# Attention: TensorE does the scores of the next pair of heads in front of the transposes of the exponentials

## The chip, the core and the metric

The kernel runs on one core of a Trainium2 chip. The metric is device time in microseconds (us). Three runs of the kernel before gave 1885.36, 1885.52 and 1888.36 us; their median is 1885.52 us.

## The reference

One layer of an encoder is applied to two sequences, a prompt of 512 tokens and a sample of 1024, width 1024. Half of the width goes through a Fourier mix, the other half through attention in a neighbourhood on a grid of 64 columns, with 8 heads of 64 channels. Then come an output projection and a gated feed-forward part. Only the attention matters here:

```python
s = jnp.einsum('bqhd,brqkhd->bqhrk', qi, kc,
               preferred_element_type=jnp.float32) * scale + bias[None]
p = jax.nn.softmax(s.reshape(b, GRID_W, h, kh * WIN_COLS), axis=-1)
p = p.reshape(b, GRID_W, h, kh, WIN_COLS).astype(v.dtype)
return jnp.einsum('bqhrk,brqkhd->bqhd', p, vc)
```

Each query sees 8 rows by 16 columns of keys; the scores get a learned bias, a softmax, and weigh the values.

## The kernel before

The kernel is five stages, one after the other, each a block in which every engine has its own hand-written list of work: first stage, projections, attention, Fourier mix, second half. Engines meet through counting semaphores alone, and each engine takes its list strictly in the order in which it is written.

`attention` (L748) works in 48 units. A unit `w` is a pair of heads, a strip of 16 columns and a chunk of 512 tokens (128 queries): 4 pairs, 4 strips, 3 chunks. Pair and strip together are a "block" `m` of three units, and there are 16 blocks. The first unit of a block has 256 keys, the other two have 384. The loop on each engine has steps `s`; a step works on several units at once:

- `scores(w)` (L947, its matmul is L958) is on TensorE. The two heads of the pair write PSUM banks 0 and 1, and each head first waits until VectorE has read the same bank for unit `w-1` (semaphore `scored`, L951).
- `score(w, hh)` (L881, its operation is L887) is on VectorE. It adds mask and bias, takes the row's extreme, and writes `s_ring`. It waits for the scores in the bank, for the mask from GpSimd (L831), and for the transposes of unit `w-2`, which read the same part of the ring.
- `exp(w, hh)` (L837, L841) is on ScalarE: the exponential in place.
- `turn(w)` (L960, L967) is on TensorE: it transposes the exponentials, 128 keys at a time, into banks 2 and 3; 4 transposes for 256 keys, 6 for 384.
- `copy_pt(w)` copies the transposed exponentials out of PSUM into `pt_ring`: the first head on ScalarE (L849), the second on VectorE (L899).
- `spread(w)` (L971, L976) and `values(w)` (L981, L992) are on TensorE: the reciprocal row sums spread over the partitions, and the product with the values. `scale_out` (L907, VectorE) writes the result.
- `turn_v(m, part)` (L936, L944) on TensorE transposes the values of the next block, staged by GpSimd (L813), through bank 7. Part 0 has four tiles, part 1 two. Part 1 uses the bank again, so it waits until ScalarE has copied part 0 out (`values_ready`, L863). VectorE copies part 1 (L915).

In step `s`, ScalarE does `exp(s, 0)`, `copy_pt(s-1)`, `exp(s, 1)`, in one step of three `values_ready`, then `copy_scale(s-1)`. VectorE does the reciprocal (L892) and `copy_pt` of unit `s-1`, with the output of `s-2` between them, and then both `score(s+1, hh)`. So VectorE's list has the copy of the transposes in front of the next scores. The steps repeat with a period of three; for what follows they are called

- **A** (`s` = 3m): turns a unit of 384 keys, scores one of 384;
- **B** (`s` = 3m+1): turns one of 256, part 0 of `turn_v`, scores one of 384;
- **C** (`s` = 3m+2): turns one of 384, part 1 of `turn_v`, scores one of 256.

Of the kernel before, what the change touches and what calls it, by code (L numbers as in the profile page):

```python
# [55 lines left out]
PAIRS_A = (D_FOURIER // 128) * NB * NCH  # L56
# [691 lines left out]
def attention(nc, at, sem, banks, kept):  # L748
# [28 lines left out]
    def pair_unit(w):  # L777
        p, b, c = w // (NB * NCH), w // NCH % NB, w % NCH
        return p, b, c, KEY_ROWS[c], KEY_ROWS[c] * KCOLS

    def block_at(s, lead):

        m, rest = divmod(s + lead, NCH)
        return m if rest == 0 and 0 < m < BLOCKS else None
# [4 lines left out]
    with nc.Block() as block:  # L789
        @block.sync  # L790
        def _(sp):
            for b in range(NB // 2, NB):
                sp.dma_start(mask[1][:, b - NB // 2], masks[:, MASK_COLS * b:MASK_COLS * b + MASK_COLS]
                             ).then_inc(mask_in[b], 16)
            for p in range(1, FT):
                if p >= 2:
                    sp.wait_ge(masked_bias, 2 * NB * NCH * (p - 1))
                load_bias(sp, rpb_pad, bias[p % 2], bias_in[p % 2], p)
                if p == 1:
                    for r, cols in enumerate((slice(0, T_PROMPT), slice(T_PROMPT, T))):  # L800
                        sp.dma_start(kept.u[:, :, cols], kept.u_scratch[:, cols].rearrange("(g p) t -> p g t", p=128)
                                     ).then_inc(kept.u_in[r], 16)
                    sp.dma_start(kept.cs[:], kept.dft_c).then_inc(kept.cs_in, 16)
                    sp.dma_start(kept.wf[:], kept.w_fmix.rearrange("g c d -> c g d")).then_inc(kept.wf_in, 16)
# [129 lines left out]
        @block.tensor  # L934
        def _(pe):
            def turn_v(m, part):  # L936
                if part:
                    pe.wait_ge(v_act, m + 1)
                else:
                    pe.wait_ge(v_staged, m + 1)  # L940
                    if m:
                        pe.wait_ge(v_dve, m)
                for t in range(4 * part, NVT if part else 4):
                    last = pe.transpose(banks[:, 7, 128 * (t % 4):128 * (t % 4) + 128], v_pair[:, m % 2, 128 * t:128 * t + 128], ident[:])  # L944
                last.then_inc(v_turned, 1)

            def scores(w):  # L947
                p, b, c, rows, n = pair_unit(w)
                for hh in range(2):
                    if w:  # L950
                        pe.wait_ge(scored, 2 * w + hh - 1)  # L951
                    head = slice(64 * hh, 64 * hh + 64)
                    q0 = p * T + c * CH + 128 * b
                    queries = z[head, q0:q0 + 128]
                    k0 = (FT + p) * T + KEY_TOKEN0[c]
                    keys = z[head, k0:k0 + rows * GRID_W].rearrange("p (r w) -> p r w", w=GRID_W)[
                        :, :, KEY_COL[b]:KEY_COL[b] + KCOLS]
                    pe.matmul(banks[:, hh, 0:n], queries, keys, start=True, stop=True).then_inc(qk_done, 1)  # L958

            def turn(w):  # L960
                rows = pair_unit(w)[3]
                for hh in range(2):
                    pe.wait_ge(exped, 2 * w + hh + 1)
                    if w:
                        pe.wait_ge((pt_act, pt_dve)[hh], w)
                    for j in range(rows // 4):
                        last = pe.transpose(banks[:, 2 + hh, 128 * j:128 * j + 128],  # L967
                                            s_ring[:, w % 2, hh, 128 * j:128 * j + 128], ident[:])
                    last.then_inc(p_turned, 1)

            def spread(w):  # L971
                pe.wait_ge(recip_done, w + 1)
                if w:
                    pe.wait_ge(scale_copied, w)
                for hh in range(2):
                    last = pe.matmul(banks[64 * hh:64 * hh + 64, 6, 0:128],  # L976
                                     stats[:, 2, 2 * w + hh:2 * w + hh + 1].broadcast_to((128, 64)), ident[:],
                                     start=True, stop=True)
                last.then_inc(scale_spread, 1)

            def values(w):  # L981
                p, b, c, rows, n = pair_unit(w)
                if c == 0:
                    pe.wait_ge(v_act, NB * p + b + 1)
                    pe.wait_ge(v_dve, NB * p + b + 1)
                pe.wait_ge(pt_act, w + 1)
                pe.wait_ge(pt_dve, w + 1)
                if w >= 2:
                    pe.wait_ge(o_done, w - 1)
                for j in range(rows // 4):  # L990
                    for hh in range(2):
                        last = pe.matmul(banks[64 * hh:64 * hh + 64, 4 + w % 2, 0:128],  # L992
                                         v_tok[:, b * NVT + V_TILE0[c] + j, 64 * hh:64 * hh + 64],
                                         pt_ring[:, w % 2, hh, 128 * j:128 * j + 128], start=(j == 0), stop=(j == rows // 4 - 1))
                last.then_inc(pv_done, 1)
            scores(0)
            turn_v(0, 0)
            turn_v(0, 1)
            for s in range(PAIRS_A + 1):
                if s:  # L1000
                    turn(s - 1)
                for part in range(2):
                    m = block_at(s, 2 - part)
                    if m is not None:
                        turn_v(m, part)
                if s + 1 < PAIRS_A:
                    scores(s + 1)
                if s:
                    spread(s - 1)
                    values(s - 1)  # L1010
# [865 lines left out]
```

## Time and profile before

| what | us |
|---|---|
| median of three runs | 1885.52 |
| the profiled execution, its own time | 1885.33 |
| span of the profiled execution | 1883.5 |
| TensorE busy in that span | 1792.1 (95%) |
| VectorE, ScalarE, GpSimd busy | 853.6, 485.9, 489.0 |
| attention stage, from 398 to 554 | 156.0 |
| TensorE, ScalarE, GpSimd, VectorE busy in that stage | 133.69, 99.29, 97.40, 89.26 |

The span runs from the first to the last instruction; 1.83 us lie around it. An engine's busy time is the union of its instructions; TensorE's overlaps of matmuls on different rows of its array are counted once. A timeline row merges neighbouring instructions of one line; its idle time stands in brackets, with what ended it. In such a row the matmul counts are of passes: a product of fp32 operands takes two, a transpose one.

### The profile page before, as it was taken

The numbers are of one execution on the slowest core, as the hardware profiler recorded it, in microseconds if no ns is written. First come the engines' busy times: TensorE is split into PE (matmuls) and PEld (weight loads), VectorE is DVE, ScalarE is ACT, GpSimd is POOL, SyncE is SP. The second block draws the span as 40 slices with busy tenths as digits, with TensorE's granted clock in tenths as the row PEclk, the third lists the DMA queues.
The fourth block names the chain that finished last, engine by engine and source line by source line (L and its number), as shares of the span: only waits on it lengthen the run. The fifth ranks groups of instructions, "written<-read, shape, count | busy, mean of one in ns | idle before, by whom it ended". The sixth has DMA issues, their size and how long they took to land.

```text
span 1883.5 us, 23423 instructions
## 1 busy us (share of the span) xinstructions
PE 1792.1 (95%) x9057; PEld 1441.0 (77%) x9057; DVE 853.6 (45%) x1292; ACT 485.9 (26%) x851; POOL 489.0 (26%) x431
## 2 busy tenths in 40 slices
PE   7599999998888899799999999999999999999999
PEld 2466888865555899678888888888888888888887
DVE  2744688225567443734243333434252525251515
ACT  3533233246655222730111111111111010111110
POOL 0300122046634232204031221313040505050504
PEclk9799999999999899899999999999999999999999
DMA  9264010341120510000101010111111101111113
GB/s 335 90 216 164 23 34 23 73 115 23 14 68 12 201 34 24 23 23 23 45 23 45 22 37 30 33 33 33 33 33 33 33 23 33 33 33 33 33 33 134
DMA packets 110374, 108.78 MB, mean 58 GB/s; under 512 B 19335, under 2 KB 87137, under 8 KB 110185
## 3 DMA queue, kind: packets, MB, share of 16 engines
q1 hardware_dynamic: 109353, 104.82, 18.4%
q0 software_dynamic: 960, 3.15, 0.4%
q8 instruction: 39, 0.64, 0.1%
q14 instruction: 22, 0.18, 0.0%
HBM read 98.50 MB, written 9.45 MB: 57 GB/s over the span
## 4 chain that ended last, share of the span: by engine, by line
PE 64%; DVE 2%; ACT 1%; issue 0%; ACTq 0%
PE banks L97 21%; PE banks L98 21%; PE banks L99 21%; DVE h_lo L1642 0%; DVE xn L1632 0%; DVE h_hi L1639 0%; PE banks L1706 0%; ACT t_second L1523 0%; ACT banks L1496 0%; PE banks L1735 0%; DVE mix_ring L1623 0%; DVE mix_ring L1620 0%; DVE wff_lo L1449 0%; ACT wff_hi L1445 0%; DVE ff_scratch L1598 0%
## 5 line engine op out<-in xcount | busy, mean ns | idle before, releaser
L1700 POOL TENSOR_TENSOR x<-x,ff_scratch 128x512 f32<-128x512 f32 x198 | 263.2, 1360 | 833.3 <-DVE ff_scratch L1598 832.7
L97 PE MATMUL banks<-h_hi,wff_hi 128*128 128x512 f32 x1056 | 413.8, 392 | 10.5 <-POOL h_lo L1687 5.7
L98 PE MATMUL banks<-h_lo,wff_hi 128*128 128x512 f32 x1056 | 412.0, 390 | 0.0
L99 PE MATMUL banks<-h_hi,wff_lo 128*128 128x512 f32 x1056 | 412.0, 390 | 0.0
L1449 DVE TENSOR_TENSOR wff_lo<-wff_raw,wff_hi 128x1024 fp32r<-128x1024 f32 x66 | 80.8, 1225 | 405.9 <-ACT wff_hi L1445 405.8
L97 PEld LDWEIGHTS banks<-h_hi,wff_hi 128*128 128x128 f32 x1056 | 198.9, 188 | 51.7 <-issue 8.8
L99 PEld LDWEIGHTS banks<-h_hi,wff_lo 128*128 128x128 f32 x1056 | 199.0, 188 | 41.4
L98 PEld LDWEIGHTS banks<-h_lo,wff_hi 128*128 128x128 f32 x1056 | 199.0, 188 | 40.4
L1598 DVE TENSOR_TENSOR ff_scratch<-banks,gate 128x512 f32<-128x512 f32 x264 | 176.9, 687 | 71.6 <-PE banks L99 49.8
L97 PE MATMUL banks<-wff_hi,ff_hi 128*128 128x512 f32 x528 | 205.4, 389 | 0.0
L98 PE MATMUL banks<-wff_lo,ff_hi 128*128 128x512 f32 x528 | 205.4, 389 | 0.0
L99 PE MATMUL banks<-wff_hi,ff_lo 128*128 128x512 f32 x528 | 205.4, 389 | 0.0
L1445 ACT ACTIVATE wff_hi<-wff_raw 128x1024 fp32r<-128x1024 f32 x66 | 70.0, 1060 | 440.7 <-DMA wff_raw<-in_w_up 353.6
L97 PE MATMUL banks<-h_hi,win_hi 128*128 128x512 f32 x384 | 151.9, 396 | 11.1 <-DVE win_lo L506 10.3
L98 PE MATMUL banks<-h_lo,win_hi 128*128 128x512 f32 x384 | 151.4, 394 | 0.0
L99 PE MATMUL banks<-h_hi,win_lo 128*128 128x512 f32 x384 | 151.1, 394 | 0.0
L99 PEld LDWEIGHTS banks<-wff_hi,ff_lo 128*128 128x128 f32 x528 | 99.1, 188 | 20.6
L97 PEld LDWEIGHTS banks<-wff_hi,ff_hi 128*128 128x128 f32 x528 | 99.1, 188 | 20.6
L98 PEld LDWEIGHTS banks<-wff_lo,ff_hi 128*128 128x128 f32 x528 | 99.1, 188 | 20.5
L97 PE MATMUL banks<-wo_hi,h_hi 128*128 128x256 f32 x384 | 110.1, 287 | 0.0
L98 PE MATMUL banks<-wo_lo,h_hi 128*128 128x256 f32 x384 | 109.7, 286 | 0.0
L99 PE MATMUL banks<-wo_hi,h_lo 128*128 128x256 f32 x384 | 109.6, 285 | 0.0
(173 smaller groups left out, 2301.0 us busy)
## 6 DMA issues: line engine op xcount, KB each, us to landing
ada_raw<-in_w_ada SPq DMA_DIRECT2D x16, 1024.0 KB, 6.6
wff_raw<-in_w_gate SPq DMA_DIRECT2D x22, 512.0 KB, 4.5
wff_raw<-in_w_up SPq DMA_DIRECT2D x22, 512.0 KB, 3.9
wff_raw<-in_w_down SPq DMA_DIRECT2D x22, 512.0 KB, 3.3
ada<-in_w_ada SPq DMA_DIRECT2D x4, 2048.0 KB, 13.0
win_raw<-in_w_in SPq DMA_DIRECT2D x16, 512.0 KB, 3.8
x_first<-in_x_sample SPq DMA_DIRECT2D x2, 2048.0 KB, 18.5
wo_raw<-in_w_o SPq DMA_DIRECT2D x4, 1024.0 KB, 9.2
```

The costliest lines, as they stand in the source:

```text
L97: pe.matmul(out, lhs[0], rhs[0], start=start, stop=False)
L98: pe.matmul(out, lhs[0], rhs[1], start=False, stop=False)
L99: return pe.matmul(out, lhs[1], rhs[0], start=False, stop=stop)
L1445: act.activation(w_hi[:, i % 3], w_raw[:, i % 3], ACT.Copy).then_inc(w_split_hi, 1)
L1449: dve.tensor_tensor(w_lo[:, i % 3], w_raw[:, i % 3], w_hi[:, i % 3].bitcast(F32), ALU.subtract).then_inc(w_ready, 1)
L1598: dve.tensor_tensor(scratch[:, n % 3], banks[:, (6 + n) % 8], gate2[:, REQ[t // 4], 512 * half:512 * half + 512], ALU.mult).then_inc(d_gat ...
L1700: pool.tensor_tensor(part, part, scratch[:, n % 3], ALU.add).then_inc(d_added, 1)
```

## The change

In TensorE's step, `scores(s + 1)` is moved from behind the transposes (`turn` and `turn_v`) to the head of the step. No instruction is added or taken away, and the lists of the other engines stay as they are.

```diff
             for s in range(PAIRS_A + 1):
+                if s + 1 < PAIRS_A:
+                    scores(s + 1)
                 if s:
                     turn(s - 1)
                 for part in range(2):
                     m = block_at(s, 2 - part)
                     if m is not None:
                         turn_v(m, part)
-                if s + 1 < PAIRS_A:
-                    scores(s + 1)
                 if s:
                     spread(s - 1)
                     values(s - 1)
```

TensorE's list in a step C before, with the semaphores that each instruction waits for (`v_act` is ScalarE's copy of the values, `exped` the exponential):

```order
L967 MATMUL banks<-ident,s_ring 128x128 [waits pt_act,exped]
L967 MATMUL banks<-ident,s_ring 128x128 x2
L967 MATMUL banks<-ident,s_ring 128x128 [waits pt_dve,exped]
L967 MATMUL banks<-ident,s_ring 128x128 x2
L944 MATMUL banks<-ident,v_pair 128x128 [waits v_act]
L944 MATMUL banks<-ident,v_pair 128x128
L958 MATMUL banks<-z 128x256 [waits scored] x2
L976 MATMUL banks<-ident,stats 64x128 [waits scale_copied,recip_done]
L976 MATMUL banks<-ident,stats 64x128
L992 MATMUL banks<-pt_ring,v_tok 64x128 [waits o_done,pt_dve,pt_act]
L992 MATMUL banks<-pt_ring,v_tok 64x128 x5
```

and the same step now:

```order
L958 MATMUL banks<-z 128x256 [waits scored] x2
L967 MATMUL banks<-ident,s_ring 128x128 [waits pt_act,exped]
L967 MATMUL banks<-ident,s_ring 128x128 x2
L967 MATMUL banks<-ident,s_ring 128x128 [waits pt_dve,exped]
L967 MATMUL banks<-ident,s_ring 128x128 x2
L944 MATMUL banks<-ident,v_pair 128x128 [waits v_act]
L944 MATMUL banks<-ident,v_pair 128x128
L976 MATMUL banks<-ident,stats 64x128 [waits scale_copied,recip_done]
L976 MATMUL banks<-ident,stats 64x128
L992 MATMUL banks<-pt_ring,v_tok 64x128 [waits o_done,pt_dve,pt_act]
L992 MATMUL banks<-pt_ring,v_tok 64x128 x5
```

The two score matmuls, with their wait for `scored`, stand ahead of the six transposes and of the wait for `v_act`, instead of behind both.

TensorE's list over a step A and the beginning of a step B, as one piece of the difference:

```order
+L958 MATMUL banks<-z 128x384 x2
 L967 MATMUL banks<-ident,s_ring 128x128 x6
+L976 MATMUL banks<-ident,stats 64x128 x2
+L992 MATMUL banks<-pt_ring,v_tok 64x128 x6
 L958 MATMUL banks<-z 128x384 x2
-L976 MATMUL banks<-ident,stats 64x128 x2
-L992 MATMUL banks<-pt_ring,v_tok 64x128 x6
 L967 MATMUL banks<-ident,s_ring 128x128 x4
```

Before, a step read transposes, scores, spread, values; now it reads scores, transposes, spread, values, so that the scores of the next step follow the values directly.

## Rows read from the trace of the kernel before

**Rows 1.** Busy time by stage (windows): attention, then Fourier; columns stand in the first line.

```profile
core 0: us, PE busy (x) PEld busy (x) DVE busy (x) ACT busy (x) POOL busy (x), PEclk, DMA share, GB/s
...
398.00:554.00 156.00, 133.69 (x1248) 89.53 (x1248) 89.26 (x352) 99.29 (x305) 97.40 (x112) 1.00 0.25 46
554.00:626.00 72.00, 55.02 (x240) 36.83 (x240) 61.60 (x71) 36.60 (x57) 26.39 (x15) 0.91 0.16 52
```

**Rows 2.** Waits of TensorE from 398 to 554: total us, times, longest us.

```profile
PE banks L944 <- ACT v_tok L863: 20.7, 16, 1.3
```

**Rows 3.** Timeline of TensorE, steps C, A, B of one block: start us, us.

```profile
472.23 0.87 PE L967 MATMUL banks<-ident,s_ring 128*128 128x128 f32 x6
474.44 0.44 PE L944 MATMUL banks<-ident,v_pair 128*128 128x128 f32 x2 [1.33 <-ACT v_tok L863]
474.81 0.70 PE L958 MATMUL banks<-z 64*128 64x256 f32 x4
475.44 0.44 PE L976 MATMUL banks<-ident,stats 128*64 128x128 f32 x4
475.71 0.83 PE L992 MATMUL banks<-pt_ring,v_tok 128*64 128x128 f32 x12
476.46 0.88 PE L967 MATMUL banks<-ident,s_ring 128*128 128x128 f32 x6
...
479.14 0.66 PE L967 MATMUL banks<-ident,s_ring 128*128 128x128 f32 x4
479.63 0.60 PE L944 MATMUL banks<-ident,v_pair 128*128 128x128 f32 x4
480.16 0.92 PE L958 MATMUL banks<-z 64*128 64x384 f32 x4
481.01 0.44 PE L976 MATMUL banks<-ident,stats 128*64 128x128 f32 x4
...
481.81 0.87 PE L967 MATMUL banks<-ident,s_ring 128*128 128x128 f32 x6
```

**Rows 4.** Timeline of ScalarE in the same steps.

```profile
472.13 0.62 ACT L841 ACTIVATE s_ring<-s_ring,stats 128x384 f32<-128x384 f32 x1
...
472.82 0.49 ACT L849 ACTIVATE pt_ring<-banks 128x384 f32<-128x384 f32 x1
473.20 0.61 ACT L841 ACTIVATE s_ring<-s_ring,stats 128x384 f32<-128x384 f32 x1
...
473.80 0.59 ACT L863 ACTIVATE v_tok<-banks 128x512 f32<-128x512 f32 x1
...
477.05 0.49 ACT L849 ACTIVATE pt_ring<-banks 128x384 f32<-128x384 f32 x1 [0.36 <-PE banks L967]
```

**Rows 5.** Timeline of VectorE in the same steps.

```profile
475.54 0.42 DVE L887 CUSTOM_DVE_ANT_0 s_ring<-banks,m_ring 128x256 f32<-128x256 f32 x1 [1.84 <-PE banks L958]
...
475.89 0.42 DVE L887 CUSTOM_DVE_ANT_0 s_ring<-banks,m_ring 128x256 f32<-128x256 f32 x1
...
476.24 0.42 DVE L915 COPY v_tok<-banks 128x256 f32<-128x256 f32 x1
476.57 0.15 DVE L892 RECIPROCAL stats<-stats 128x2 f32<-128x2 f32 x1
...
477.38 0.56 DVE L899 COPY pt_ring<-banks 128x384 f32<-128x384 f32 x1 [0.46 <-PE banks L967]
...
479.83 0.42 DVE L899 COPY pt_ring<-banks 128x256 f32<-128x256 f32 x1 [0.28 <-PE banks L967]
...
481.11 0.56 DVE L887 CUSTOM_DVE_ANT_0 s_ring<-banks,m_ring 128x384 f32<-128x384 f32 x1 [0.85 <-PE banks L958]
...
481.59 0.55 DVE L887 CUSTOM_DVE_ANT_0 s_ring<-banks,m_ring 128x384 f32<-128x384 f32 x1
482.07 0.08 DVE L887 DVE_READ_ACCUMULATOR2_ANT stats<- 128x1 f32 x1
```

**Rows 6.** TensorE's weight loads at the stage's start, the second head alone, then transposes.

```profile
401.48 0.29 PEld L958 LDWEIGHTS banks<-z 64*128 64x128 f32 x2 [0.71 <-DVE stats L887]
402.32 0.20 PEld L967 LDWEIGHTS banks<-ident,s_ring 128*128 128x128 f32 x2 [0.55 <-ACT s_ring L841]
```

## The prediction

> **What bounds the kernel now.** I read the busy time by stage first. The change touches one stage, attention, of 156.00 us, in which TensorE is busy for 133.69 us and no other engine for 100 [rows 1]. Then the waits: TensorE's one large wait there is part 1 of `turn_v` on ScalarE's copy of the values, 20.7 us in 16 times [rows 2]. Then the timeline of one block. Step C takes 476.46 − 472.23 = 4.23 us, A 2.68, B 2.67, together 9.58, and within A and B each group of TensorE starts where the one before it ends [rows 3]. So TensorE sets the pace in A and B, and in C it stands for 1.33 us with the next scores queued behind the wait. VectorE is waiting for these scores: 1.84 us in C, 0.85 in B [rows 5]. That is the gap which the new order can fill.
>
> The second reading is how far the loop from engine to engine is from binding. Before, `scores(s+1)` comes behind `turn(s-1)`, and its banks were emptied by VectorE at the end of step s-1. Between the transposes of one step and the scores that need VectorE's work on them lie a whole step of TensorE's own. Nothing waits for `scored` in these three steps.
>
> **What the change does to the loop.** Number and kind of instructions stay the same on all engines; DMA, GpSimd and the queue of SP keep their lists, and GpSimd's mask for a unit needs `scored` of two units before, a step earlier than anything here. What changes is who stands behind whom. In a new step s the scores wait for VectorE's `score(s, hh)`; `turn(s-1)` waits behind them; VectorE's list has `copy_pt(s-1)`, which needs `turn(s-1)`, in front of `score(s+1)`; and `score(s+1, 1)` releases the next step's scores. Scores, transposes, copy, two scores on VectorE, scores: this circle now closes once per step, and spread and values no longer help to fill it, since they run beside VectorE's part.
>
> Its length, from the start of the second head's scores to the next such start, in **step A**:
> - scores of 384 keys, second head alone, to the transposes: 402.32 − 401.48 = 0.84 [rows 6]; the pair together takes 481.01 − 480.16 = 0.85 [rows 3], so that a head that starts later is not shortened;
> - six transposes, start to VectorE's copy: 477.38 − 476.46 = 0.92 [rows 3, 5];
> - copy of 384, start to the next operation of VectorE: 0.56 busy less the overlap with the next. The copy of 256 has 476.57 − 476.24 = 0.33 for 0.42 busy, an overlap of 0.09, so 0.47 [rows 5];
> - first score to second: 481.59 − 481.11 = 0.48; second to its last instruction's end: 482.07 + 0.08 − 481.59 = 0.56 [rows 5];
> - from an engine's end to TensorE's start: 474.44 − (473.80 + 0.59) = 0.05 [rows 3, 4].
>
> Sum 3.32 us, against 2.68 before: +0.64. TensorE's own work fits in beside it: 0.84, then 0.92, the copy's whole 0.56 and 0.05, for which `values` waits, and 476.46 − 475.71 = 0.75 of values make 3.12 [rows 3, 5].
>
> **Step B** turns four tiles and copies 256: transposes to copy 479.83 − 479.14 = 0.69, copy 0.33 [rows 3, 5]. So 0.84 + 0.69 + 0.33 + 0.48 + 0.56 + 0.05 = 2.95, against 2.67: +0.28.
>
> **Step C** scores 256 keys, which take 475.44 − 474.81 = 0.63 [rows 3]. VectorE's circle is 0.63 + 0.92 + 0.47 + 0.35 + 0.42 + 0.05 = 2.84 [rows 3, 5], and does not decide. TensorE still needs the values' copy for `turn_v`, and that copy stands behind `copy_pt` in ScalarE's list, which needs the transposes. From the start of the transposes: 477.05 − 476.46 = 0.59 to `copy_pt`; then copy, exponential, values' copy, and the start of `turn_v`: 474.44 − 472.82 = 1.62; then 474.81 − 474.44 = 0.37 to the next group and 476.46 − 475.44 = 1.02 of spread and values [rows 3, 4]. With the scores in front: 0.63 + 0.59 + 1.62 + 0.37 + 1.02 = 4.23. The same as before. The scores have left the place behind the wait, but the transposes that the wait hangs on have moved back by as much. Before, ScalarE had just ended its first exponential when the transposes of the first head were there: 472.23 + 0.59 = 472.82, its copy's start [rows 3, 4]. There was no slack to take up the delay.
>
> The change of step A counts 15 times (s = 3 to 45), of B 16 times (s = 1 to 46), of C nothing: 15 × 0.64 + 16 × 0.28 = 14.1 us. The stage behind starts when attention has ended, so all of it reaches the end: 1885.33 + 14.1 = 1899.4, and against the median, 0.2 us higher, **1899.5 us**.
>
> Prices that the trace of before doesn't show. VectorE's copy directly followed by a score: between 0.47 and 0.56 for 384 (0.33 and 0.42 for 256), the upper end if nothing overlaps: +0.09 in 31 steps, +2.8 us; I keep 0.47, by the one pair of neighbours on VectorE that starts with such a copy. TensorE going from values to scores and from transposes to spread directly: I take 0.20 after the last start, as between values and transposes now. It matters in C alone; at 0.11, a pass among its like, both together give −0.18 × 15 = −2.7 us; at 0.41, which is what scores need before another group, the first gives +0.21 × 15 = +3.2. So the sum lies between +11.4 and +20.1.
>
> **The rivals.** *Faster: the wait in C takes the scores in.* If the transposes reached ScalarE no later than now, C would lose 0.63, and if A and B stayed bound by TensorE the whole would be −0.63 × 15 = −9.5: 1876.0. For it speaks that the wait is twice as long as the scores (1.33 against 0.63) [rows 3]. It decides where ScalarE's copy has 0.63 us of slack behind the transposes; it has none [rows 4]. The Trainium skill ("Perfetto Trace Analysis", section "Optimization Strategy") advises to find the gaps of the most contended engine and to make what ends them start sooner; read as filling the gap, it gives this rival. Chance 0.07.
>
> *No change: the circle stays hidden.* That would need the copy and both scores of VectorE to end behind spread, values and part 0 of `turn_v`. In A the circle would have to be 0.64 us shorter than its rows, in B 0.28. Then 1885.5. Chance 0.06.
>
> *Slower still: the clock falls.* Attention has a granted clock of 1.00, so 2.4 GHz throughout. In the Fourier stage behind it, where TensorE stands for 17 of 72 us, the mean is 0.91, which is 18% of the time at 1.2 GHz [rows 1]. The new stage would stand for 170 − 134 = 36 of 170 us. At the same 18%, with TensorE's scores and transposes some half of the circle, it would cost 170 × 0.18 × 0.5 = 15 us more: 1915. Against it: the longest gap of TensorE stays what it is, 0.59 + 1.62 less some 0.7 of transposes, about 1.5 us [rows 3, 4], and 16 gaps of 1.3 us leave the clock at 1.00 now [rows 1, 2]. Chance 0.05.
>
> **How the numbers follow.** The forecast has 0.80, its own range being 1896.7 (+11.4) to 1905.4 (+20.1); I widen it to 1893 and 1907, since each step's sum hangs on differences of a few hundredths and the runs of before spread over 3 us upward. The remaining 0.02 is for what I don't see, on the slower side. Below 1893 lie the first two rivals, above 1907 the third: 0.2 left out in all. A measurement of this kernel can tell about 0.2%, 3.8 us, from no change; all of the forecast's range is beyond that. So faster 0.07, same 0.06, slower 0.87.
>
> **What would show it.** In the changed kernel a block takes some 10.5 us instead of 9.58, A 3.3, B 2.95, C 4.2. TensorE gets a new wait at L958 on VectorE (`stats`, L887), about twice per block, and one at L992 for the copy L899 in step A; its wait at L944 on `v_tok` stays, with 1.3 to 1.6 us. VectorE's wait at L887 for L958 is gone; it waits at L899 for L967 instead, longer than now. Busy times stay, the stage grows from 156 to about 170 us, and the other stages keep theirs. I am wrong if the wait at L944 is under 0.9 us, if no wait at L958 stands in A and B, or if the clock of the stage is under 1.00.

## The result and the profile after

The changed kernel takes 1904.38 us in the median of four runs (1902.53 to 1905.30), the kernel before 1885.58 us (1885.36 to 1888.36). The ratio is 1.0095, with a 95% interval of 1.0078 to 1.0113: slower by about 18.8 us. The profiled execution took 1902.53 us of its own, 17.2 us more than that of before.

The windows by stage, as in [rows 1]: busy time of TensorE, its weight loads, VectorE, ScalarE, GpSimd, then the granted clock.

```profile
398.00:570.00 172.00, 144.21 (x1248) 94.15 (x1248) 89.46 (x352) 98.27 (x305) 97.38 (x112) 1.00 0.23 42
570.00:642.00 72.00, 56.11 (x240) 37.90 (x240) 60.41 (x71) 36.60 (x57) 25.22 (x15) 0.89 0.16 52
```

The attention stage has grown from 156 to 172 us with the same instructions, at the same clock of 1.00. From the first scores to the first matmul of the Fourier stage it takes 172.1 us instead of 156.2: +15.9.

The waits that answer to [rows 2], for TensorE, and one each of VectorE's and ScalarE's (total us, times, longest us), after:

```profile
PE banks L944 <- ACT v_tok L863: 20.7, 16, 1.3
PE banks L992 <- issue: 5.6, 17, 0.3
DVE pt_ring L899 <- PE banks L967: 60.9, 48, 1.5
ACT pt_ring L849 <- PE banks L967: 52.0, 48, 1.6
```

and the last three of them before:

```profile
PE banks L992 <- issue: 0.7, 2, 0.3
DVE pt_ring L899 <- PE banks L967: 16.8, 47, 0.5
ACT pt_ring L849 <- PE banks L967: 6.5, 16, 1.1
```

The wait on the values' copy has not lost a tenth of a microsecond: 20.7 us in 16 times, as before. TensorE has a new one in front of the product with the values (5.6 us for 0.7), and both copying engines wait far longer for the transposes (60.9 us for 16.8, and 52.0 for 6.5).

TensorE's timeline over steps A, B, C of one block, the rows that answer to [rows 3]:

```profile
484.64 0.92 PE L958 MATMUL banks<-z 64*128 64x384 f32 x4
485.49 0.87 PE L967 MATMUL banks<-ident,s_ring 128*128 128x128 f32 x6
486.30 0.44 PE L976 MATMUL banks<-ident,stats 128*64 128x128 f32 x4
487.06 0.88 PE L992 MATMUL banks<-pt_ring,v_tok 128*64 128x128 f32 x12 [0.33 <-issue]
487.87 1.01 PE L958 MATMUL banks<-z 64*128 64x384 f32 x4
488.81 0.66 PE L967 MATMUL banks<-ident,s_ring 128*128 128x128 f32 x4
489.30 0.60 PE L944 MATMUL banks<-ident,v_pair 128*128 128x128 f32 x4
489.83 0.44 PE L976 MATMUL banks<-ident,stats 128*64 128x128 f32 x4
490.18 0.66 PE L992 MATMUL banks<-pt_ring,v_tok 128*64 128x128 f32 x8
490.77 0.86 PE L958 MATMUL banks<-z 64*128 64x256 f32 x4
491.56 0.88 PE L967 MATMUL banks<-ident,s_ring 128*128 128x128 f32 x6
493.77 0.44 PE L944 MATMUL banks<-ident,v_pair 128*128 128x128 f32 x2 [1.33 <-ACT v_tok L863]
494.14 0.44 PE L976 MATMUL banks<-ident,stats 128*64 128x128 f32 x4
...
495.16 0.92 PE L958 MATMUL banks<-z 64*128 64x384 f32 x4
496.01 0.88 PE L967 MATMUL banks<-ident,s_ring 128*128 128x128 f32 x6
```

From transposes to transposes A takes 488.81 − 485.49 = 3.32 us, B 2.75, C 4.45, together 10.52; the median over all blocks is 10.51, before 9.58. Scores of 384 keys end 0.85 after the second head's start, those of 256 after 0.63, so from second head to second head the steps are 3.32, 2.97 and 4.23.

VectorE in the same steps, which answers to [rows 5]:

```profile
486.40 0.56 DVE L899 COPY pt_ring<-banks 128x384 f32<-128x384 f32 x1 [1.35 <-PE banks L967]
486.88 0.55 DVE L887 CUSTOM_DVE_ANT_0 s_ring<-banks,m_ring 128x384 f32<-128x384 f32 x1
...
487.35 0.55 DVE L887 CUSTOM_DVE_ANT_0 s_ring<-banks,m_ring 128x384 f32<-128x384 f32 x1
487.83 0.08 DVE L887 DVE_READ_ACCUMULATOR2_ANT stats<- 128x1 f32 x1
```

Here is the circle, link by link: transposes at 485.49, VectorE's copy at 486.40, its two scores at 486.88 and 487.35, the second done at 487.91. TensorE had started the next scores at 487.87 with the first head; the second head had to wait for that 487.91, which shows as 1.01 us of scores where 0.92 is the rule, and not as idle time. In A the circle is the longer of two paths by only these 0.09 us: the other one, on which the product waits for VectorE's copy, brought the first head to 487.87.

### The profile page after: what moved, and what is told of

It is laid out like the page before. It is cut to its first block, busy times and chain, and to the rows that moved or that the text cites. A ratio compares the mean times of both kernels' runs of the same rounds, so it can differ in the third digit from the quotient of the medians.

```text
span 1900.7 us, 23423 instructions
## 1 busy us (share of the span) xinstructions
PE 1804.2 (95%) x9057; PEld 1447.0 (76%) x9057; DVE 852.7 (45%) x1292; ACT 485.0 (26%) x851; POOL 488.6 (26%) x431
## 4 chain that ended last, share of the span: by engine, by line
PE 64%; DVE 2%; ACT 1%; issue 0%; ACTq 0%
PE banks L97 21%; PE banks L98 21%; PE banks L99 21%; DVE h_lo L1642 0%; DVE xn L1632 0%; DVE h_hi L1639 0%; PE banks L1706 0%; ACT t_second L1523 0%; ACT banks L1496 0%; PE banks L1735 0%; DVE mix_ring L1623 0%; DVE mix_ring L1620 0%; DVE wff_lo L1449 0%; ACT wff_hi L1445 0%; DVE ff_scratch L1598 0%
```

## The experiments

Times are medians; the ratio is against runs of the kernel before made alongside, whose median is between 1885.6 and 1887.3 us. "Block" is the median of A + B + C from transposes to transposes in the trace, "stage" the time from the first scores to the first matmul of the Fourier stage, all in us.

| kernel | time | against before (95%) | block | stage |
|---|---|---|---|---|
| before | 1885.6 to 1887.3 | 1 | 9.58 | 156.2 |
| changed | 1904.4 | 1.0095 (1.0078 to 1.0113) | 10.51 | 172.1 |
| e1_between | 1880.1 | 0.9968 (0.9956 to 0.9979) | 9.10 | 149.4 |
| e2_extra_after | 1927.3 | 1.0221 (1.0204 to 1.0238) | 11.49 | 196.3 |
| e3_extra_before | 1886.6 | 1.0003 (0.9993 to 1.0012) | 9.58 | 156.2 |
| e4_values_first | 1864.0 | 0.9879 (0.9862 to 0.9895) | 8.03 | 135.2 |
| e5_only_a | 1895.3 | 1.0050 (1.0033 to 1.0067) | 10.13 | 164.5 |
| e6_only_b | 1893.1 | 1.0034 (1.0021 to 1.0046) | 9.88 | 165.2 |
| e7_only_c | 1895.6 | 1.0051 (1.0033 to 1.0069) | 9.97 | 165.0 |
| e8_start | 1904.0 | one run | 10.51 | 173.3 |
| e9_values_first_after | 1885.7 | 0.9994 (0.9984 to 1.0004) | 9.29 | 155.3 |
| e10_between_values_first | 1869.8 | 0.9911 (0.9895 to 0.9928) | 8.33 | 137.8 |
| e11_after_again | 1902.5 | one run | 10.51 | 172.1 |
| e12_start_again | 1905.1 | one run | 10.51 | 173.3 |

**Is it VectorE's circle?** One useless operation of VectorE was put on the suspected circle, in the changed kernel and in the one before. It writes a tile that nothing reads.

```diff
                 if 1 <= s <= PAIRS_A:
                     copy_pt(s - 1)
+                    dve.memset(spare[:, s % 2], 0.0)
                 if s + 1 < PAIRS_A:
                     score(s + 1, 0)
```

> The changed kernel with one useless operation of VectorE per step, a memset of 512 columns, between its copy of the transposes and its scores. A memset of 256 columns takes 0.27 us at L1194, so about 0.54 us. Theory (circle): the operation lies on the circle in A and B and beside ScalarE's chain in C: 31 x 0.54 = 17 us over the changed kernel, about 1921 us, blocks of 11.6 us. Rival (TensorE pays for the sequence of its groups): VectorE has time to spare, so nothing: 1904 us.

> The same useless operation of VectorE, about 0.54 us per step, in the kernel before. Theory (circle): in the old order VectorE's scores have a step of TensorE's as slack, so it costs nothing: 1885.5 us, blocks of 9.58 us. If VectorE's list itself were what decides, 48 x 0.54 = 26 us more: 1911 us.

The operation's group in the first of the two, from the costliest groups of VectorE (count, busy us, mean ns, idle before):

```profile
L928 DVE MEMSET spare<- 128x512 f32 x48 | 23.3, 485 | 2.7
```

It took 0.485 us, a little less than the 0.54 estimated. Behind the changed order a block grew by 0.98 us, twice that length: A from 3.32 to 3.80, B from 2.75 to 3.24, C not at all (4.45). The transposes of steps B, C, A and B of this kernel, at a clock of 1.00:

```profile
427.17 0.65 PE L969 MATMUL banks<-ident,s_ring 128*128 128x128 f32 x4
...
430.41 0.87 PE L969 MATMUL banks<-ident,s_ring 128*128 128x128 f32 x6
...
434.85 0.88 PE L969 MATMUL banks<-ident,s_ring 128*128 128x128 f32 x6
...
438.66 0.66 PE L969 MATMUL banks<-ident,s_ring 128*128 128x128 f32 x4
```

Behind the old order (e3_extra_before) the block stayed at 9.58 to a hundredth. The same work costs its whole length in A and B of the one kernel and nothing in the other. So the rival by which TensorE pays for the new sequence of its groups falls as the cause of what the changed kernel lost in A and B, and the circle stands.

The 31 steps account for 31 × 0.485 = 15 us; the median rose by 22.9 over the changed kernel, and the stage of this trace by 24.2. The rest goes with falls of the granted clock to 1.2 GHz, five in this stage: one at its start, from 398.0 to 408.2 us, and four inside. The next window, with one of them, has the mean 0.86 where the changed kernel has 1.00:

```profile
475.00:500.00 25.00, 21.70 (x156) 13.74 (x154) 13.49 (x50) 12.42 (x38) 11.71 (x14) 0.86 0.36 32
```

In the four blocks in which the inner falls lie, C takes 5.9 to 6.3 us instead of 4.45.

**Is the order of scores and transposes what matters?** The scores were put between `turn` and `turn_v`, so that they pass the wait but not the transposes.

```diff
                 if s:
                     turn(s - 1)
+                if s + 1 < PAIRS_A:
+                    scores(s + 1)
                 for part in range(2):
                     m = block_at(s, 2 - part)
                     if m is not None:
                         turn_v(m, part)
-                if s + 1 < PAIRS_A:
-                    scores(s + 1)
```

> The scores stand between turn and turn_v in TensorE's step: transposes first, as in the kernel before, but the scores are not behind the wait of turn_v. Theory (the circle scores, transposes, VectorE's copy, VectorE's scores closes once per step only if the scores stand in front of the transposes): A and B stay at 2.68 and 2.67 us, C loses the 0.63 us of scores that then run inside the wait, a block takes 8.95 us, the whole 15 x 0.63 = 9.5 us less than before: 1876 us. No wait at L958 for VectorE. Rival (TensorE itself pays, for another sequence of groups and for scores that are no longer followed by spread): scores are followed by another group than before in B and C, so two thirds of the 0.93 us per block that the changed kernel lost stay, and the gain in C is used up: about 1885 us.

It is faster than the kernel before, by 6 us. C takes 3.60 us, exactly 0.63 less; A stays at 2.67. TensorE's wait on the values' copy is halved:

```profile
PE banks L944 <- ACT v_tok L863: 11.2, 16, 0.7
```

B went from 2.67 to 2.83 where nothing was expected, 2.7 us over the stage, which is the gap between the 9.5 us forecast and the 6.8 us by which the stage shrank. The rows of a step C, A and B of this kernel:

```profile
477.90 0.88 PE L967 MATMUL banks<-ident,s_ring 128*128 128x128 f32 x6
...
481.50 0.87 PE L967 MATMUL banks<-ident,s_ring 128*128 128x128 f32 x6
...
484.18 0.66 PE L967 MATMUL banks<-ident,s_ring 128*128 128x128 f32 x4
484.77 0.92 PE L958 MATMUL banks<-z 64*128 64x384 f32 x4
485.61 0.66 PE L944 MATMUL banks<-ident,v_pair 128*128 128x128 f32 x4
486.20 0.44 PE L976 MATMUL banks<-ident,stats 128*64 128x128 f32 x4
```

In B the scores start 0.59 us after the transposes, where `turn_v` started 0.49 after them [rows 3], and spread starts 0.59 after `turn_v`, where the scores came 0.53 after it. TensorE's list of waits has none in these places, so this looks like a price of the sequence itself, and a small part of the rival holds for this order. The scores can fill the wait, as the change's idea has it; what spoils it is that they also stand ahead of the transposes.

**What does each step cost alone?** The new order in one step of three, the old one in the other two; for A:

```diff
+                if s % 3 == 0 and s + 1 < PAIRS_A:
+                    scores(s + 1)
                 if s:
                     turn(s - 1)
...
-                if s + 1 < PAIRS_A:
+                if not (s % 3 == 0) and s + 1 < PAIRS_A:
                     scores(s + 1)
```

and with `s % 3 == 1` for B, `s % 3 == 2` for C.

> Scores in front of the transposes in step A alone (s = 3m), B and C in the old order. Theory (circle): without the next step in the new order the circle does not close; what A loses is TensorE's own wait, since the transposes come 0.85 us later and the product with the values must wait for VectorE's copy of them: 0.85 + 0.92 + 0.56 + 0.05 + 0.75 = 3.13 us against 2.68, +0.45 in 15 blocks: 1892 us; a new wait at L992 for L899, none at L958. Rival (every changed step costs the same 0.31 us by a worse sequence of TensorE's groups): +0.31 x 15 = 4.7, no wait at L992: 1890 us.

> Scores in front of the transposes in step B alone (s = 3m+1). Theory (circle): the second head's scores wait some 0.17 us for VectorE, part 0 of turn_v covers VectorE's copy of the transposes, B takes 0.17 + 0.84 + 1.02 + 0.80 = 2.83 us against 2.67, +0.16 in 16 blocks: 1888 us, a wait at L958 for L887. Rival (the same 0.31 us per changed step): +5: 1890.5 us.

> Scores in front of the transposes in step C alone (s = 3m+2). Theory (circle): VectorE's scores of the step B before end late, so the second head waits 0.39 us, and ScalarE's chain to the values' copy starts that much later; the 0.63 us of scores come off behind the wait and go on in front of it: C takes 0.39 more, 15 x 0.39 = 5.9 us: 1891 us; the wait at L944 stays 1.3 us. Rival (the wait takes the scores in): C loses 0.63, 1876 us. Rival (0.31 us per changed step): 1890 us, without a wait at L958.

Per block A alone costs 0.55 us, B 0.30, C 0.39, together 1.25 and thus more than all three at once (0.93): each alone has a wait of its own, and in the full change they lie side by side. C is the forecast's 0.39 to the hundredth, with the wait where it was looked for: the scores of a step C of this kernel, where a pair of 256 keys takes 0.70 in the old order [rows 3], and the VectorE rows whose end, 444.23, the second head awaits:

```profile
443.89 1.09 PE L958 MATMUL banks<-z 64*128 64x256 f32 x4
444.92 0.88 PE L967 MATMUL banks<-ident,s_ring 128*128 128x128 f32 x6
```

```profile
443.67 0.55 DVE L887 CUSTOM_DVE_ANT_0 s_ring<-banks,m_ring 128x384 f32<-128x384 f32 x1
444.15 0.08 DVE L887 DVE_READ_ACCUMULATOR2_ANT stats<- 128x1 f32 x1
```

A was to cost 0.45 and has the wait in front of the product with the values, 5.6 us in 17 times, as the changed kernel has. So most of the 0.64 us that A loses in the changed kernel is lost without the circle, by this wait alone; the circle adds the last 0.09. B was to cost 0.16 and cost 0.30, which by its size alone could be the rival's 0.31. Its scores take 1.09 us where 0.92 is the rule, so 0.17 are the second head's wait, as forecast; the rest is behind. In its trace spread follows `turn_v` at once, values come 0.34 after spread where 0.27 was the rule, and take 0.59 to the next group, not 0.53. The product starts 0.25 us after VectorE's copy ended, at 487.56; before it stands a wait for five semaphores. In e1_between, where the same wait stands but the copy had ended over a microsecond earlier, values come 0.27 after spread. This looks like the price of a wait for several semaphores of which one comes late, but no run takes them apart. Against the kernel before measured alongside (1886.7 us) the times of these three lie 0.3, 1.5 and 3.0 us above what their blocks give; the trace of e7_only_c has two falls of the clock inside attention, that of e6_only_b one at its start.

**What holds C?** On ScalarE the copy of the values was put first in its step; TensorE's order was once the old one, once the changed one, once that of e1_between.

```diff
             for s in range(PAIRS_A + 1):
+                m = block_at(s, 1)
+                if m is not None:
+                    values_ready(m)
                 if s < PAIRS_A:
                     exp(s, 0)
                 if s:
                     copy_pt(s - 1)
                 if s < PAIRS_A:
                     exp(s, 1)
-                m = block_at(s, 1)
-                if m is not None:
-                    values_ready(m)
```

> The kernel before, TensorE's order untouched; on ScalarE the copy of the values (L863) comes first in its step, before both exponentials and the copy of the transposes. Theory (C's wait at L944 stands at the end of ScalarE's chain copy, exponential, values' copy): TensorE's wait of 1.33 us in C goes, C takes about 2.9 us, a block about 8.25 us, the whole 15 x 1.33 = 20 us less: 1865 us. Rival (ScalarE's exponentials come 0.6 us later and the next transposes wait for them instead): the wait moves to L967, and less than half of the 20 us is gained: 1876 to 1886 us.

> The changed kernel with ScalarE's copy of the values first in its step, as in e4_values_first. Theory: this frees C alone of ScalarE's chain; the circle through VectorE stays and sets the pace: A 3.32, B 2.97, C 0.63 + 0.92 + 0.56 + 0.10 + 0.75 = 2.96 us (scores, transposes to VectorE's copy, the copy, its hand-over, the product with the values), a block 9.25 us instead of 10.51: 15 x 1.26 = 19 us less than the changed kernel, about 1885 us, and 20 us more than e4_values_first, which has the old order. Rival (what the changed order costs hangs on the wait at L944 alone): with the wait gone, old and new order are alike, 1864 us.

> e4_values_first with the scores between turn and turn_v, as in e1_between. Theory (TensorE sets the pace in all three steps once the wait at L944 is gone): moving the scores has nothing to fill any more and only changes which groups follow each other; B keeps the 0.15 us that it lost in e1_between, so 1864 to 1869 us, not under e4_values_first. Rival (both gains add up: 22 and 6 us): 1858 us.

With the old order of TensorE this is the fastest kernel of the study: 1864.0 us, 22 us under the kernel before. A, B and C take 2.67, 2.67 and 2.68 us. C was to take about 2.9: the wait's 1.33 us are counted from the end of the last transpose, but `turn_v`, which started 2.21 us after the first transpose of C [rows 3], now starts 0.72 after it, and the next group 0.31 after that, not 0.37:

```profile
480.01 0.87 PE L967 MATMUL banks<-ident,s_ring 128*128 128x128 f32 x6
480.73 0.38 PE L944 MATMUL banks<-ident,v_pair 128*128 128x128 f32 x2
481.04 0.70 PE L958 MATMUL banks<-z 64*128 64x256 f32 x4
```

TensorE has no gap left in the middle of the stage (windows, the columns of [rows 1]):

```profile
475.00:500.00 25.00, 25.00 (x243) 17.39 (x241) 17.11 (x68) 18.58 (x59) 19.30 (x23) 1.00 0.01 2
```

The wait stood at the end of ScalarE's list in that step and at nothing else; the data had been there since step B. With the changed order the same edit brings a block of 9.29 us (expected 9.25) and 1885.7 us (expected 1885): A and B keep their 3.32 and 2.97, because their circle never came by ScalarE. Old and new order stand 21.6 us apart with the wait gone in both. And with the wait gone, the scores between `turn` and `turn_v` fill nothing: 1869.8 us, just above the 1864 to 1869 expected, and 0.30 us per block behind e4_values_first, half in B and half in C. The gains do not add up; the wait could be taken away once.

**The start and the clock.** The stage has grown by 15.9 us. From the first transposes to the last it takes 162.4 us instead of 148.5, +13.9, where the forecast's sum has 14.1; the other 2.0 us lie in front of the first transposes. At the stage's start the changed kernel shows (TensorE, then VectorE):

```profile
400.63 1.91 PE L958 MATMUL banks<-z 64*128 64x384 f32 x4
402.71 1.87 PE L958 MATMUL banks<-z 64*128 64x384 f32 x4 [0.18 <-DVE stats L887]
404.51 0.66 PE L967 MATMUL banks<-ident,s_ring 128*128 128x128 f32 x4
```

```profile
402.09 0.56 DVE L887 CUSTOM_DVE_ANT_0 s_ring<-banks,m_ring 128x384 f32<-128x384 f32 x1 [0.18 <-POOL m_ring L831]
```

The scores of unit 2 wait for VectorE's scores of unit 1, those for GpSimd's first masks, and the first transposes stand behind: they start 6.46 us after the first scores, where the kernel before has 4.42. To take that apart, the old order was kept in the first two steps:

```diff
+                if s >= 2 and s + 1 < PAIRS_A:
+                    scores(s + 1)
                 if s:
                     turn(s - 1)
...
-                if s + 1 < PAIRS_A:
+                if not (s >= 2) and s + 1 < PAIRS_A:
                     scores(s + 1)
```

> The changed kernel with the old order in the first two steps (s = 0 and 1), the new one from s = 2 on. It is read from the trace alone. In the changed kernel the first transposes start 6.46 us after the first scores, in the kernel before 4.42 us: the scores of unit 2 wait for VectorE's scores of unit 1, which wait for GpSimd's first masks, and the transposes of unit 0 stand behind that. Theory: with the old order there the first transposes start at 4.4 us again and the attention stage is 1 to 2 us shorter than the changed kernel's 172.07 us. Rival (the start's delay is taken up in the steps behind it): 172 us.

> e8_start once more: the changed kernel with the old order in the first two steps. In e8_start the clock stood at 1.2 GHz from 399.9 to 406.7 us, in the very steps it was to measure. Theory: where the clock is 1.00 there, the first transposes start 4.4 us after the first scores, and the stage is 1 to 2 us shorter than 172.07 us. Rival: 172 us.

> The changed kernel once more, for one trace: whether steps and stage repeat and where the granted clock falls. Theory: A 3.32, B 2.75 and C 4.45 us from transposes to transposes, stage 172.1 us. If its runs above 1904 us have a fall of the clock inside attention, this shows as a stretch at 1.2 GHz there; if the runs differ by the Fourier stage, as 77.75 against 78.82 us.

The kernel with the old start, run twice, gave no answer. In both its traces the granted clock stood at 1.2 GHz for 6.8 us in just these steps (399.7 to 406.5 us in e8_start). The window of e12_start_again, and behind it that of the changed kernel:

```profile
398.00:413.00 15.00, 12.19 (x68) 7.42 (x70) 6.08 (x25) 8.18 (x22) 12.83 (x15) 0.77 1.03 216
```

```profile
398.00:413.00 15.00, 12.40 (x80) 7.02 (x80) 6.46 (x26) 8.57 (x23) 12.78 (x15) 1.00 1.09 215
```

The first transposes came 5.2 us after the first scores, against 6.5 in the changed kernel and 4.4 in the one before, and the stage took 173.3 us, longer rather than shorter.

Other kernels of this study do answer. In e5_only_a the first two steps are in the old order in effect (in `s` = 0 no transposes stand behind the scores), and its granted clock is 1.00 through the stage:

```profile
396.93 0.70 PE L958 MATMUL banks<-z 64*128 64x256 f32 x4 [0.95 <-PEq L428]
401.35 0.66 PE L967 MATMUL banks<-ident,s_ring 128*128 128x128 f32 x4
```

Its first transposes come 4.42 us after the first scores, and its stage grew by 8.3 us, which its 15 blocks account for with 15 × 0.55, so that nothing is left for a start. e7_only_c, with both first steps in the old order, also has 4.42. The changed kernel, run once more, has 6.47 and repeated itself otherwise: 1902.54 us, steps and stage to a hundredth or two. So the 2.0 us at the start belong to the new order in these steps. That putting the old order back there, and nothing else, returns them at a clock of 1.00 is not shown.

## Why the prediction was right, step by step

It said 1899.5 us, 1893 to 1907; measured were 1904.4. The way and the mechanism came as forecast. That the time lies inside the range is in part luck: the prices by which the sum could grow to +20.1 came out as taken, and the 4.9 us above the forecast have other sources, named under "The size".

- **TensorE sets the pace before, and the scores can run in its gap.** Shown by e1_between and e4_values_first: 0.63 us less in C by the one, the whole gap by the other.
- **The circle closes once per step.** A was to take 3.32 us and takes 3.32, B 2.95 and takes 2.97, C 4.23 and takes 4.23. e2 and e3 show that it is this circle: VectorE's work costs its length in A and B of the new order and nothing in the old. In A it was a near thing. The prediction has TensorE's own work, with the product's wait for VectorE's copy, at 3.12 us; it came to 3.23, since the product starts 0.10 after the copy's end (486.96, 487.06), not 0.05, and the next scores 0.81 after the product, not 0.75. Without the circle A would still have lost 0.55, as e5_only_a shows.
- **C gains nothing.** Its parts are as summed: 493.77 − 491.56 = 2.21 from transposes to `turn_v` (0.59 + 1.62), 0.37 to spread, 1.02 to the next scores. The scores went from behind the wait to in front of the transposes that the wait hangs on; 20.7 us of wait before and after. e9 shows it from the other side: with ScalarE's chain gone, C comes down to 9.29 − 3.32 − 2.97 = 3.00 us, and only C.
- **The prices that were bounded.** VectorE's copy followed by a score: 486.88 − 486.40 = 0.48, at the lower end of 0.47 to 0.56, as taken. The two gaps of TensorE in C were together 1.39 us as taken (0.37 + 1.02).
- **The size.** The sum is 14.1 us, against 17.2 in the profiled execution. Its steps hold: from the first transposes to the last the stage grew by 13.9. The step that failed is that the sum begins with the steps, as if the way to the first transposes stayed as it was, and sets GpSimd's masks aside as a step earlier. At the start VectorE's scores wait for the first masks, and the transposes of unit 0 now stand behind that: 6.46 us instead of 4.42, 2.0 that the sum lacks. A further 1.1 us lie in the Fourier stage, from its first matmul to the last one of L1706: 77.7 us before, 78.8 after, with a mean clock of 0.89 for 0.91. This need not come from the change: e3_extra_before, whose attention stage is as long as that of before, has 79.0 us there. The median lies 1.6 us more above its profiled execution than that of before does; no trace of those runs exists, and this stays open.
- **What was to be seen in the profile.** The waits were right in kind, but not all in the list. The second head's wait at L958 hides in the first head's work and appears as 1.01 us of scores; the list has no such wait in A and B. The rule that I gave for being wrong, no wait at L958, would have misled; the start of the next scores beside VectorE's end would not.

The rivals. That the wait takes the scores in: false, with 20.7 us of wait unchanged; it becomes true when the scores stay behind the transposes. By the Trainium skill ("Perfetto Trace Analysis", section "Optimization Strategy") one finds what a gap waits for and makes that start sooner: e4_values_first does just this and gains 22 us, while moving work into the gap gained 6 at best. That the circle stays hidden: false by e2. That the clock falls: not in the changed kernel, which kept 1.00 through attention in both its traces. Falls there do occur and cost time: in e2_extra_after, whose circle is 0.49 us longer, some 9 us of the stage beside the 15. That more standing of TensorE brings them, as this rival has it, is not shown: e7_only_c has two falls inside attention with TensorE busy for 142.6 of 164.9 us, the changed kernel none with 144.2 of 172.0.

## What to carry to other kernels

In an engine's fixed list, work moved forward past something that another engine waits for can turn a dependence of two steps into a circle of one; add up that circle link by link, from rows, before anything else. Here the gap was better closed at what ends it (22 us) than filled (6 us): the wait was for a copy that stood last in ScalarE's list though its data had been ready for a step. And where a second matmul runs beside a first one, its wait does not show as idle time, so look at starts and lengths as well as at the list of waits.

## What the runs showed of the hardware

The granted clock fell at the stage's start in some traces and not in others: to 1.2 GHz for 6.8 us in e4_values_first, e8_start, e9_values_first_after and e12_start_again and for 10.2 us in e2_extra_after and e6_only_b, where the kernel before and both traces of the changed one had 1.00 in the same steps. In e8_start and e12_start_again every engine's list is that of the kernel before up to the fall, so that the order of the work in this stage does not explain it; what does stays open. Of two heads on different rows of the array, the second was held by its semaphore while the first ran on to its end: 1.91 us for both at 400.63, where a pair together takes 0.92.
